# Value products of two heads, alternated key block by key block, in a hybrid attention and retention trunk

## The reference

```python
qx, kx, vx = qkv(hx)          # 16 heads of 64
qz, kz, vz = qkv(hz)
s_lat = einsum('bqhd,bkwhd->bhqkw', qr, kb) * scale + bias   # learned bias, masked outside the window
s_ctx = einsum('bqhd,bnhd->bhqn', qr, kz) * scale
p = softmax(concatenate([s_lat, s_ctx], axis=-1))
out = einsum('bhqkw,bkwhd->bqhd', p_lat, vb) + einsum('bhqn,bnhd->bqhd', p_ctx, vz)
```

## Time and profile before

| | us |
|---|---|
| median of three runs | 2822.44 |
| lowest and highest | 2821.64, 2827.18 |
| the profiled execution | 2820.71 |
| its span | 2818.9 |
| TensorE busy, and share of the span | 2463.0, 87% |
| VectorE | 1390.6, 49% |
| GpSimd | 1026.6, 36% |
| ScalarE | 934.7, 33% |

### The profile page before, as it was taken

One profiled execution on the slowest core, in us unless ns is written; L12 is line 12 of the kernel. 1 busy time (PEld: TensorE's weight loads), 2 busy tenths in 40 slices (PEclk: granted clock), 3 DMA queues, 4 the chain that ended last, 5 costly groups with the idle time before them and its releaser, 6 DMA issues.

```text
span 2818.9 us, 34589 instructions
## 1 busy us (share of the span) xinstructions
PE 2463.0 (87%) x11378; PEld 1962.6 (70%) x11378; DVE 1390.6 (49%) x2238; ACT 934.7 (33%) x1517; POOL 1026.6 (36%) x431
## 2 busy tenths in 40 slices
PE   0638878999989999998999989997999998776998
PEld 0525556887867776687888867666788786655998
DVE  7996747766132322115766132444866413565441
ACT  2215433222222333223223223443322223344553
POOL 1212223444433332243444434212344443223786
PEclk9869989999999999999999999999999999998999
DMA  7331113654222221123654227221555422212443
GB/s 275 142 134 45 45 35 136 227 202 173 93 82 77 79 70 58 69 90 128 229 202 172 103 69 145 72 69 36 219 204 194 147 92 82 68 60 75 147 165 135
DMA packets 116395, 341.28 MB, mean 121 GB/s; under 512 B 34929, under 2 KB 36209, under 8 KB 115697
## 3 DMA queue, kind: packets, MB, share of 16 engines
q1 hardware_dynamic: 90896, 330.81, 32.9%
q10 hardware_dynamic: 25440, 9.72, 2.0%
HBM read 335.80 MB, written 4.69 MB: 121 GB/s over the span
## 4 chain that ended last, share of the span: by engine, by line
issue 50%; POOL 19%; PE 19%; DVE 9%; ACT 2%; DMA 1%; POOLq 0%; DVEq 0%; SPq 0%; ACTq 0%
POOL w_lo L413 19%; PE low_banks L420 14%; PE high_banks L420 5%; DVE dump L1055 3%; DVE rot L1174 1%; DVE rot L1176 1%; ACT e_x L799 1%; DVE tmp L1132 0%; DVE ssum_rstd L1119 0%; ACT e_z L805 0%; DVE h_lo L1143 0%; DMA ada_first<-in_ada_w 0%; DVE kT L1177 0%; DVE mod L1063 0%; ACT lnm L759 0%
## 5 line engine op out<-in xcount | busy, mean ns | idle before, releaser
L413 POOL TENSOR_TENSOR w_lo<-w_raw,w_hi 128x1024 fp32r<-128x1024 f32 x424 | 1026.1, 2431 | 1771.5 <-ACT w_hi L740 1771.0
L420 PE MATMUL low_banks<-h_hi,w_hi 128*128 128x512 f32 (+1 forms) x1664 | 622.8, 374 | 46.5 <-DVE h_lo L1143 23.2
L740 ACT ACTIVATE w_hi<-w_raw 128x1024 fp32r<-128x1024 f32 x424 | 444.6, 1057 | 565.2 <-PE low_banks L420 315.8
L420 PE MATMUL low_banks<-h_lo,w_hi 128*128 128x512 f32 (+1 forms) x1664 | 617.3, 371 | 0.0
L420 PE MATMUL low_banks<-h_hi,w_lo 128*128 128x512 f32 (+1 forms) x1664 | 616.9, 371 | 0.0
L420 PEld LDWEIGHTS low_banks<-h_hi,w_hi 128*128 128x128 f32 x1664 | 319.0, 192 | 111.1 <-issue 49.6
L1055 DVE SCALAR_TENSOR_TENSOR ssum_rstd<-ada_raw,high_banks 128x1024 f32<-128x1024 f32 x288 | 351.1, 1219 | 24.8 <-DMA ada_raw<-in_ada_w 17.3
L420 PEld LDWEIGHTS low_banks<-h_lo,w_hi 128*128 128x128 f32 x1664 | 319.1, 192 | 52.4 <-issue 1.0
L420 PEld LDWEIGHTS low_banks<-h_hi,w_lo 128*128 128x128 f32 x1664 | 318.5, 191 | 53.1
L969 ACT ACTIVATE lnm<-low_banks 128x512 f32<-128x512 f32 (+1 forms) x88 | 47.9, 544 | 421.3 <-PE low_banks L420 421.3
L1105 DVE SCALAR_TENSOR_TENSOR xT<-low_banks,mod,xT 128x256 f32 (+1 forms) x84 | 36.7, 476 | 282.6 <-PE low_banks L420 282.6
(11 more groups left out here) (172 smaller groups left out, 3733.6 us busy)
## 6 DMA issues: line engine op xcount, KB each, us to landing
w_raw<-in_weights SPq DMA_DIRECT2D x424, 512.0 KB, 3.3
ada_raw<-in_ada_w SPq DMA_DIRECT2D x144, 512.0 KB, 3.7
ada_rest<-in_ada_w SPq DMA_DIRECT2D x8, 2048.0 KB, 7.7
ada_first<-in_ada_w SPq DMA_DIRECT2D x4, 2048.0 KB, 14.7
bias<-rpb_skew ACTq DMA_DIRECT2D x64, 64.0 KB, 2.4
rpb_skew<-rpb_rows ACTq DMA_DIRECT2D x1, 3556.0 KB, 37.2
cond_l<-in_cond SPq DMA_DIRECT2D x3, 1024.0 KB, 4.4
xT<-in_xT SPq DMA_DIRECT2D x1, 2048.0 KB, 14.7
```

Of the source, the lines that this page charges most:

```text
L413: nc.gpsimd.tensor_tensor(out=w_lo[:, r, :], in0=w_raw[:, r, :], in1=w_hi[:, r, :], op=ALU.subtract).then_inc(lo_ready, 1)
L420: return nc.tensor.matmul(dst, lhsT, rhs, start=start, stop=stop, **kw)
L740: nc.scalar.activation(w_hi[:, r, :], w_raw[:, r, :], ACT.Copy).then_inc(hi_ready, 1)
```

## The change

The loop over the two heads moves inside the loop over key blocks. Each head's wait for its nT copies stays ahead of that head's first product. With one head the order is the old one.

```diff
-                def values_product(t, sub):
-
-                    pe.wait_ge(L.aT_ready, t * L.groups + per * (sub + 1))
-                    lo, hi = (64 * sub, 64 * sub + 64) if L.na else (0, P)
+                def values_product(t):
+
                     for j, kb in enumerate((2, 3, 0, 1)):
                         if kb >= 2 and L.zq:
                             g, a, w = kb - 1, 0, TOK
                         else:
                             g, a, w = kb // 2, (kb % 2) * SEQ, SEQ
-                        mov = (nT[:, sub, g, a:a + w] if L.na else aT[:, g, a:a + w])
-                        last = mm(bank[6][lo:hi, 0:w], v_st[:, kb, lo:hi], mov, j == 0, j == 3)
+                        for sub in range(subs):
+                            if j == 0:
+
+                                pe.wait_ge(L.aT_ready, t * L.groups + per * (sub + 1))
+                            lo, hi = (64 * sub, 64 * sub + 64) if L.na else (0, P)
+                            mov = (nT[:, sub, g, a:a + w] if L.na else aT[:, g, a:a + w])
+                            last = mm(bank[6][lo:hi, 0:w], v_st[:, kb, lo:hi], mov, j == 0, j == 3)
                     return last
 
                 def back(t):
...
                     pe.wait_ge(L.vst_ready, t + 1)
-                    for sub in range(subs):
-                        last = values_product(t, sub)
-                    last.then_inc(L.pv_done, 1)
+                    values_product(t).then_inc(L.pv_done, 1)
```

## The result

| | us |
|---|---|
| before, median of 20 runs (lowest, highest) | 2823.08 (2817.04, 2829.46) |
| after, median of 20 runs (lowest, highest) | 2828.51 (2823.48, 2831.89) |
| ratio, with its 95% interval | 1.0015 (1.0008 to 1.0022) |

The ratio puts the change at 0.0015 x 2823 = 4.2 us slower, between 2.3 and 6.2. It is a small loss, clear of noise. The two medians alone lie 5.4 us apart; I go by the ratio, because it has an interval. The forecast was +3.5.

What follows compares the result with a forecast made beforehand. Layer 2 was taken as bound by a chain from nT copies through ScalarE's conversion and GpSimd's subtractions to L1188. Terms: -1.0 (last tile) + 4.5 (clock) = +3.5 us, on the median 2822.4 giving 2825.9 us; range 2820.5 to 2829.5.

Steps and rivals of the forecast that it cites:

- The chain: Layer 2, tiles 1 to 7: mask add L1188 ends only after GpSimd's subtractions, so earlier value products gain 0.
- The overlap: Value products: alternating heads run fully side by side on TensorE, 0.9 us less per tile, 1.0 in the last.
- The serial rival: Alternating heads' value passes run one by one, today's overlap lost: +4.3 us, 2826.7 us; chance 0.08.
- The new wait: Head 1's first value product waits for the last nT copy, 0.83 us after the first product, covered by head 0's.
- The price of the longer wait: TensorE's wait before the transposes grows from 1.7 to 2.6 us in six tiles; clock may halve: +4.5 us.
- falls: Clock drops to half level as transposes resume after TensorE's wait; three in six tiles forecast, 1.5 us each.
- two nearby rows: Profile waits of TensorE: after 2.10 us the clock was at half level, after 3.38 us it was not.
- The last tile: The output projection follows the last tile's value products on TensorE at once, so 1.0 us is kept.
- Full gain: Rival: value products are on the chain, so every layer 2 tile gets shorter; 7.3 us faster, 2815.1 us; chance 0.10.
- The case of every tile cold: Rival: all six waits bring the half level for the whole of the transposes; +11.2 us, 2833.6 us; chance 0.10.

Runs made afterwards that it cites:

- late conversion: Changed order, with ScalarE converting layer 2's two weight units after y_hi instead of before; ratio to the kernel before 0.9966, median 2816.32 us.
- early mask: Mask added to the bias right after the copy of k; ratio to the kernel before 0.9959 with the old order, 0.9932 with the alternation.
- old_shortened: Kernel before, with four of the k unit's 24 matmuls left out in tiles 2 to 8; ratio to the kernel before 1.0013, median 2831.73 us.
- new_padded: Changed kernel, with four extra matmuls ahead of the k unit in tiles 2 to 8; ratio to the kernel before 0.9993, median 2824.71 us.
- new_padded_half: Changed kernel, with two extra matmuls ahead of the k unit in tiles 2 to 8; ratio to the kernel before 1.0012, median 2826.59 us.

## Why the prediction was right

The forecast was 2825.9 us with a range from 2820.5 to 2829.5, and the measured median is 2828.51. Against the 20 runs of before the change is 4.2 us, where +3.5 was forecast. Step by step:

- **The chain.** "L1188 ends where it does" held in all seven tiles: it took 2.1 to 2.64 us, where it took 1.22 to 1.75, and the next instruction began 7.6 to 7.7 us after the first value product as before. The reading that carried it was that three tiles had different starts and one end. The late conversion and the early mask confirm it from two sides.
- **The overlap.** The last pass was forecast 3.30 us after the first, 3.2 in the last tile; measured 3.28 to 3.30 and 3.17. In the second tile a wide pass of each head begins at 1786.58 and 1786.59, and the next pair 0.43 us later, the pace that one head alone had. The rule that weight loads overlap only across row groups (Trainium skill, TensorE: Matmul & The Clock Gate, "The mechanism") does not hold here: both heads use all rows, and their next weight loads begin 1 and 2 ns after these two passes, which last 0.59 us. That rule speaks of weight loads; "by it nothing overlaps" was the prediction's own step from it. The serial rival is out.
- **The new wait.** Head 1's first product waits for the last nT copy and nothing behind it is late, as the 3.30 shows.
- **The price of the longer wait.** Forecast 3 falls of 1.5 us; the profile has 3 of 1.45. The count was a choice between two nearby rows and the exact hit is luck: old_shortened, with the same waits, had two, and the profile is of the slowest of 20 executions. The interval of the ratio, +2.3 to +6.2 us, allows a mean of 2.3 to 5.0 falls, if 1 us goes off. The two rows were single draws as well. The wait of 3.38 us after which the clock held stands at the same place in all eight profiles (3.37 to 3.40 us), and in six of them the half level set in during it, the changed kernel's among them. The range that the prediction gave its own case, 1 to 5 falls of 1 to 2 us, has its top at 2831.4 by its own terms, not at 2830.
- **The last tile.** The 1.0 us is there: 4.19 to 3.17. That it is kept is shown only up to the matmul behind the output projection, which starts 53.75 us after the last tile's first value product in the kernel before and 52.73 in the changed one. After the next wait, with TensorE at the half level in both, 0.5 us of it is left (60.23 and 59.77), and from the last tile's first value product to the end of the span the two profiles differ by 0.2 us the other way (901.6 and 901.7). Whether it reaches the end in the mean of many runs stays open.
- **The rivals.** Full gain would have needed the value products on the chain; with the mask moved they are, as a part of TensorE's own work, and it comes (6.4 + 0.9 us against the 7.3 worked out). The case of every tile cold did not come; three waits of 2.6 us kept the full level in the same profile.

What stays open is how often a wait of a given length is followed by the half level. Profiles of single executions showed 0 of 12 at 1.7 us (before, new_padded), 0 of 6 at 1.2 to 1.4, 2 of 6 at 2.1, and 5 of 12 at 2.6. That is too few for a rate. With all waits of 1.2 to 1.8 us of all eight profiles, wherever in the kernel they stand, it is 1 of 193.

## What to carry to other kernels

Before shortening an engine's work, find what ends the wait that follows it; and where an instruction's start and duration vary from tile to tile but its end keeps a fixed distance to another engine's end, that engine may be what holds it; here it was, and nothing ahead of it paid. An engine that gets idle time in place of work can end up slower, because TensorE's clock may fall: here some of the waits of 2.1 and of 2.6 us had that price and none of the six of 1.7 in the kernel before, so a saving that only lengthens a wait of TensorE is to be booked as a possible loss. When a sound local gain vanishes, keep it and move the instruction that swallows it: here the same alternation was worth 7 us once the mask add was elsewhere.

## What the runs showed of the hardware

- Extra matmuls made a kernel faster: 28 matmuls more in layer 2 took its first-to-last distance from 166.3 to 161.8 us, and the ratio to the kernel before from 1.0015 to 0.9993.
- A VectorE add with both operands in SBUF and a GpSimd subtraction there exclude each other for nearly their whole length: the add took 2.1 to 2.64 us instead of 1.22 and ended 1.08 us after GpSimd in every tile, so about 0.14 us of it ran in the overlap; the other way round GpSimd's pair took 5.58 us instead of 4.67. VectorE instructions with an operand in PSUM were not held up: y_lo took 0.69 us in the tiles with that GpSimd work and in the last tile, which has none, and the bias add 0.42 us under it.
- Code that is the same but for at most two matmuls reached the first value product at 1755.6, 1762.0, 1753.0 and 1763.6 us in four profiles (before, after, new_padded_half, new_conv_late). The granted clock goes with it: up to there it was at the half level for 167, 184, 164 and 188 us. A difference between two profiled spans is therefore no measure of a change of this size; a distance inside the touched stage is.
